# A gated recurrence with context: one accumulated state product, shorter chain, earlier place for the second direction

## The reference

```python
def hgrn2_scan(q, k, v, logf, s0, with_output):
    gcum = jnp.cumsum(chunks(logf), axis=2)
    g_end = gcum[:, :, -1]
    k_end = kc * jnp.exp(g_end[:, :, None] - gcum)
    chunk_states = jnp.einsum("bcshk,bcshv->bchkv", k_end, vc)
    s_final, s_in = lax.scan(_carry_step, s0, ...)        # s = dec * s + st
    if not with_output:
        return None, s_final
...
    q_rel = qc * jnp.exp(gcum - g_mid)
    k_rel = kc * jnp.exp(g_mid - gcum)
    att = jnp.where(causal, einsum(q_rel, k_rel), 0.0)
    o_intra = einsum(att, vc)
    o_inter = einsum(qc * jnp.exp(gcum), s_in)
    return o_intra + o_inter

# for each direction d (direction 1 on flipped tokens)
o_c, s_ctx = hgrn2_scan(qc_d, k_c, v_c, logf_c, s0, need_ctx)
o_l, _ = hgrn2_scan(q_l, k_l, v_l, logf_l, s_ctx, True)
```

## Time and profile before

| | us |
|---|---|
| median of 3 runs | 2481.95 (2480.68 to 2485.22) |
| profiled execution | 2486.94 |
| its span, first to last instruction | 2485.1 |
| rounds 3 to 7 of the loop, together | 136.10 |
| round 4 alone | 24.86 |

### The profile page before, as it was taken

One profiled execution on the slowest core, in us unless ns is written; L12 is line 12 of the kernel. 1 busy time (PEld: TensorE's weight loads), 2 busy tenths in 40 slices (PEclk: granted clock), 3 DMA queues, 4 the chain that ended last, 5 costly groups with the idle time before them and its releaser, 6 DMA issues. The chain is left out here.

```text
span 2485.1 us, 36625 instructions
## 1 busy us (share of the span) xinstructions
PE 2175.1 (88%) x12398; PEld 1790.4 (72%) x12398; DVE 1712.1 (69%) x2903; ACT 1366.1 (55%) x2135; POOL 277.2 (11%) x357
## 2 busy tenths in 40 slices
PE   5999899889998999888886799994889987799993
PEld 4899876589984666667575677783677786577782
DVE  5884626288555698977653699994478674699993
ACT  2663425166453355565333578883476652588882
POOL 0000000000000365555000001101000000001100
PEclk8999999999999999989997799996999887799996
DMA  6455431545543666400121699994221121699991
GB/s 219 162 186 170 142 109 45 203 158 190 175 135 145 250 222 239 162 1 1 43 84 51 230 389 389 390 386 177 94 77 59 52 85 60 219 394 398 393 371 68
DMA packets 127256, 454.99 MB, mean 183 GB/s; under 512 B 13824, under 2 KB 17792, under 8 KB 126976
## 3 DMA queue, kind: packets, MB, share of 16 engines
q1 hardware_dynamic: 116160, 413.14, 45.7%
q0 software_dynamic: 10944, 39.85, 4.2%
HBM read 431.97 MB, written 20.97 MB: 182 GB/s over the span
## 5 line engine op out<-in xcount | busy, mean ns | idle before, releaser
L2722 DVE TENSOR_TENSOR moe_w_lo<-ring,moe_w_hi 128x1024 fp32r<-128x1024 f32 x384 | 462.8, 1222 | 61.9 <-ACT moe_w_hi L2660 57.0
L2660 ACT CAST moe_w_hi<-ring 128x1024 fp32r<-128x1024 f32 x384 | 399.0, 1049 | 147.3 <-PE ps L236 119.4
L373 DVE TENSOR_TENSOR ffn_w_lo<-ring,ffn_w_hi 128x1024 fp32r<-128x1024 f32 x132 | 161.0, 1222 | 101.2 <-ACT ffn_w_hi L325 101.0
L234 PE MATMUL ps<-moe_w_hi,moe_own 128*128 128x512 f32 x512 | 213.8, 418 | 12.1 <-DVE moe_own L2729 11.1
L235 PE MATMUL ps<-moe_w_lo,moe_own 128*128 128x512 f32 x512 | 204.6, 400 | 0.0
L236 PE MATMUL ps<-moe_w_hi,moe_own 128*128 128x512 f32 x512 | 204.6, 400 | 0.0
L325 ACT CAST ffn_w_hi<-ring 128x1024 fp32r<-128x1024 f32 x132 | 137.4, 1044 | 107.4 <-PE ps L236 107.4
L234 PE MATMUL ps<-ffn_h_hi,ffn_w_hi 128*128 128x256 f32 x608 | 173.3, 285 | 11.2 <-DVE ffn_w_lo L373 11.2
L235 PE MATMUL ps<-ffn_h_lo,ffn_w_hi 128*128 128x256 f32 x608 | 172.0, 283 | 0.0
L236 PE MATMUL ps<-ffn_h_hi,ffn_w_lo 128*128 128x256 f32 x608 | 172.0, 283 | 0.0
L234 PE MATMUL ps<-ffn_hid,ffn_w_hi 128*128 128x256 f32 x448 | 131.1, 293 | 12.7 <-DVE ffn_w_lo L373 8.8
(11 more groups left out here) (541 smaller groups left out, 5692.0 us busy)
## 6 DMA issues: line engine op xcount, KB each, us to landing
ring<-in_weights SPq DMA_DIRECT2D x766, 512.0 KB, 5.4
expert_rows<-moe_y POOLq DMA_DIRECT2D x32, 512.0 KB, 7.1
token_rows<-moe_token_rows SPq DMA_DIRECT2D x6, 512.0 KB, 2.6
sq<-in_cmp_w SPq DMA_DIRECT2D x1, 2048.0 KB, 9.8
both<-in_x SPq DMA_DIRECT2D x1, 1024.0 KB, 5.8
both<-in_context SPq DMA_DIRECT2D x1, 1024.0 KB, 8.1
out<-both SPq DMA_DIRECT2D x1, 1024.0 KB, 4.8
cols<-in_cols SPq DMA_DIRECT2D x1, 720.5 KB, 9.1
```

What stands on the lines that cost most here:

```text
L234: pe.matmul(out, w_hi, x_hi, start=start, stop=False)
L373: dve.tensor_tensor(w_lo[:, u % WB], k.ring[:, (first + u) % RING], w_hi[:, u % WB], ALU.subtract).then_inc(w_split, 1)
L2660: act.copy(w_hi[:, j % WB].rearrange("p h f -> p (h f)"), k.slot(act, first + GU + j, e).rearrange("p a f -> p (a f)")).then_inc(w_rounded, 1)
L2722: dve.tensor_tensor(w_lo[:, j % WB].rearrange("p h f -> p (h f)"), k.ring[:, (first + GU + j) % RING].rearrange("p a f -> p (a f)"), w_hi[ ...
```

## The change

The context's state of a direction comes from one product over 256 tokens, in two accumulated matmuls of 128 tokens. For this the context's keys need the decay to the end of the context, not to the end of their chunk. `decays` therefore makes two scans: one over the latent half, restarted at each chunk, in place in `logs`, and one over 255 or 256 columns without restart that gives the decay to the end directly into `gs`; for direction 0 this second scan runs backwards through the columns, for direction 1 the first one does. The column at the end of the context is zero (cleared once). The latent half of `gs` then gets chunk end minus sum. The subtractions over 512 columns and the copy to `dec` go; `exps` reads the ends of the four latent chunks with a stride.

`carry` makes two matmuls of 128 tokens and three of 64 in place of seven of 64. `chain` makes one copy and three steps in place of one copy and six. On VectorE, `mask(h-2, 1)` and `chain(h-2, 1)` move in front of the split of `places[1]`.

```diff
@@ carry (TensorE)
+                        for a in range(2):
+                            pe.matmul(k.ps[:, STATE[0], 0:P], ket[:, d, a, :], v[:, a, h * P:(h + 1) * P], start=(a == 0), stop=(a == 1))
                         for c in order(d)[:-1]:
-                            a, r = c // 2, c % 2 * GC
-                            mm = pe.matmul(k.ps[:, STATE[c % 2], a * P:(a + 1) * P], ket[r:r + GC, d, a, :],
+                            a, r = 2 + c // 2, c % 2 * GC
+                            mm = pe.matmul(k.ps[:, STATE[c % 2], a * P - P:a * P], ket[r:r + GC, d, a, :],
                                            v[r:r + GC, a, h * P:(h + 1) * P], start=True, stop=True)
@@ exps (ScalarE)
-                        act.activation(ke[:, d, :], logs[:, d, :], ACT.Exp)
-                        act.activation(dec[:, h % 2, d, :], dec[:, h % 2, d, :], ACT.Exp)
-                        act.activation(qs[:, h % 2, d, :], gs[d][:, T:], ACT.Exp)
+                        act.activation(ke[:, d, :], gs[d][:, :], ACT.Exp)
+                        act.activation(dec[:, h % 2, d, :], chunk_ends(d), ACT.Exp)
+                        act.activation(qs[:, h % 2, d, :], logs[:, d, T:], ACT.Exp)
@@ before the loop (VectorE)
-                    dve.memset(sin[:, :, :, :], 0.0)
+                    dve.memset(gs[0][:, T - 1:T], 0.0)
+                    dve.memset(gs[1][:, 0:1], 0.0)
@@ decays (VectorE)
-                        dve.tensor_tensor_scan(gg[:, :], reset, L, 0.0, ALU.mult, ALU.add)
-                        dve.drain()
-                        chunks = gg[:, :].rearrange("p (c t) -> p c t", t=GC)
-                        dve.tensor_copy(own_dec, chunks[:, :, GC - 1])
-                        dve.drain()
-                        end = own_dec.unsqueeze(2).broadcast_to([P, 2 * NCH, GC])
+                        one = reset[:, 1:2].broadcast_to([P, T - 1])
                         if d == 0:
-                            dve.tensor_tensor(L.rearrange("p (c t) -> p c t", t=GC), end, chunks, ALU.subtract)
+                            dve.tensor_tensor_scan(sums, reset[:, T:], sums, 0.0, ALU.mult, ALU.add)
+                            dve.tensor_tensor_scan(to_end[:, 0:T - 1][:, ::-1], one, raw[:, 1:T][:, ::-1], 0.0, ALU.mult, ALU.add)
                             mid, edge = HC // 2 - 1, HC - 1
                         else:
-                            dve.tensor_tensor(L, gg[:, :], L, ALU.subtract)
-                            dve.drain()
-                            dve.tensor_tensor(chunks, end, L.rearrange("p (c t) -> p c t", t=GC), ALU.subtract)
-                            dve.drain()
+                            dve.tensor_tensor_scan(sums[:, ::-1], reset[:, T:], sums[:, ::-1], 0.0, ALU.mult, ALU.add)
+                            dve.tensor_tensor_scan(to_end[:, 1:T], one, raw[:, 0:T - 1], 0.0, ALU.mult, ALU.add)
                             mid, edge = HC // 2, HC
+                        dve.drain()
+                        dve.tensor_tensor(to_end[:, T:].rearrange("p (c t) -> p c t", t=GC), chunk_ends(d).unsqueeze(2).broadcast_to([P, NCH, GC]),
+                                          sums.rearrange("p (c t) -> p c t", t=GC), ALU.subtract)
@@ the rounds (VectorE)
-                        for n in places[1]:
-                            split(n + WB)
                         if live(h - 2):
                             mask(h - 2, 1)
                             chain(h - 2, 1)
+                        for n in places[1]:
+                            split(n + WB)
```

More of the change, by code:

```diff
@@ L2992, in odd_mixer @@
             rel = tb("hg_rel", [P, 2, 4, T])
-            dec = tb("hg_dec", [P, 2, 2, 2 * NCH])
+            dec = tb("hg_dec", [P, 2, 2, NCH])
             att = tb("hg_att", [P, 2, 2, P])
-            sin = tb("hg_s_in", [P, 2, NCH + 1, P])
+            sin = tb("hg_s_in", [P, 2, NCH, P])
             unit = tb("hg_unit", [P, 2 * GH - 1])
@@ L3024, in order, with chunk_ends @@
                 def order(d):
-                    ctx_ch = list(range(NCH))
-                    lat_ch = list(range(NCH, 2 * NCH))
-                    return (ctx_ch + lat_ch) if d == 0 else (ctx_ch[::-1] + lat_ch[::-1])
+                    return range(NCH) if d == 0 else range(NCH - 1, -1, -1)
+                def chunk_ends(d):
+                    at = GC - 1 if d == 0 else 0
+                    return logs[:, d, T:].rearrange("p (c t) -> p c t", t=GC)[:, :, at]
                 @block.sync
@@ L3110, in mix @@
                                           start=(d == 0 and a == 0), stop=False, skip_group_check=True)
-                            for i, c in enumerate(order(d)[NCH:]):
-                                cc = c - NCH
-                                mm = pe.matmul(k.ps[:, OUT, cc * GC:(cc + 1) * GC], sin[:, d, 1 + i, :],
+                            for i, cc in enumerate(order(d)):
+                                mm = pe.matmul(k.ps[:, OUT, cc * GC:(cc + 1) * GC], sin[:, d, i, :],
                                                qs[:, h % 2, d, cc * GC:(cc + 1) * GC], start=False, stop=(d == 1 and i == NCH - 1),
@@ L3334, in decays @@
                         u = 2 * h + d
-                        gg, L, own_dec = gs[d], logs[:, d, :], dec[:, h % 2, d, :]
+                        raw, to_end = logs[:, d, :], gs[d]
+                        sums = raw[:, T:]
                         dve.wait_ge(logged, u + 1)
@@ L3338, in decays @@
                             dve.wait_ge(expd, u - 1)
-                        dve.tensor_tensor_scan(gg[:, :], reset, L, 0.0, ALU.mult, ALU.add)
-                        dve.drain()
-                        chunks = gg[:, :].rearrange("p (c t) -> p c t", t=GC)
-                        dve.tensor_copy(own_dec, chunks[:, :, GC - 1])
-                        dve.drain()
-                        end = own_dec.unsqueeze(2).broadcast_to([P, 2 * NCH, GC])
+                        one = reset[:, 1:2].broadcast_to([P, T - 1])
                         if d == 0:
-                            dve.tensor_tensor(L.rearrange("p (c t) -> p c t", t=GC), end, chunks, ALU.subtract)
+                            dve.tensor_tensor_scan(sums, reset[:, T:], sums, 0.0, ALU.mult, ALU.add)
+                            dve.tensor_tensor_scan(to_end[:, 0:T - 1][:, ::-1], one, raw[:, 1:T][:, ::-1], 0.0, ALU.mult, ALU.add)
                             mid, edge = HC // 2 - 1, HC - 1
                         else:
-                            dve.tensor_tensor(L, gg[:, :], L, ALU.subtract)
-                            dve.drain()
-                            dve.tensor_tensor(chunks, end, L.rearrange("p (c t) -> p c t", t=GC), ALU.subtract)
-                            dve.drain()
+                            dve.tensor_tensor_scan(sums[:, ::-1], reset[:, T:], sums[:, ::-1], 0.0, ALU.mult, ALU.add)
+                            dve.tensor_tensor_scan(to_end[:, 1:T], one, raw[:, 0:T - 1], 0.0, ALU.mult, ALU.add)
                             mid, edge = HC // 2, HC
+                        dve.drain()
+                        dve.tensor_tensor(to_end[:, T:].rearrange("p (c t) -> p c t", t=GC), chunk_ends(d).unsqueeze(2).broadcast_to([P, NCH, GC]),
+                                          sums.rearrange("p (c t) -> p c t", t=GC), ALU.subtract)
                         for i, size, ref in ((0, GC, edge), (1, HC, mid)):
-                            own = gg[:, T:].rearrange("p (c t) -> p c t", t=size)
+                            own = sums.rearrange("p (c t) -> p c t", t=size)
                             refs = own[:, :, ref:ref + 1].broadcast_to([P, T // size, size])
@@ L3385, in chain @@
                         dve.wait_ge(states, 2 * h + d + 1)
+                        dve.tensor_copy(sin[:, d, 0, :], k.ps[:, STATE[0], 0:P])
                         for i, c in enumerate(order(d)[:-1]):
[L3387 to L3395, removed]
+                            dve.drain()
+                            ch = dve.scalar_tensor_tensor(sin[:, d, i + 1, :], sin[:, d, i, :], dec[:, h % 2, d, c:c + 1],
+                                                          k.ps[:, STATE[c % 2], (c // 2 + 1) * P:(c // 2 + 2) * P], ALU.mult, ALU.add)
                         ch.then_inc(chained, 1)
```

## The result

| | before | after |
|---|---|---|
| median, us | 2483.59 (4 runs, 2480.68 to 2486.85) | 2450.23 (4 runs, 2447.53 to 2455.03) |
| profiled execution, us | 2486.94 | 2447.53 |
| span, us | 2485.1 | 2445.8 |
| rounds 3 to 7, us | 136.10 | 109.57 |

The ratio is 0.9867, 95% interval 0.9844 to 0.9891: 33 us faster. The forecast was 2445, in a range of 2438 to 2463. (The same pair measured twice more: 0.9864, 0.9821 to 0.9908, and 0.9876, 0.9854 to 0.9897.)

What follows compares the result with a forecast made beforehand. Mix waited for VectorE's second-direction chain, late behind a split, with TensorE's low clock following the idle. Gains in rounds 2 to 9 summed to 36.8 us, giving 2450.1; minus 5.0 from profile to median, 2445, range 2438 to 2463.

Steps and rivals of the forecast that it cites:

- rounds 3 to 7: Five rounds at 21.75 us each instead of 136.10 us together, a gain of 27.35 us.
- Both halves are needed: VectorE's round: 22.65 us with the chain only moved, 23.7 with it only shortened, 18.6 us of work with both.
- round 9: The loop's round 9: a gain of 0.26 us; rounds 10 and after were to gain nothing.
- The carry: TensorE's carry with two 128-row and three 64-row products: 0.96 us, saving 0.13 per direction, 0.26 per round.
- Round 2: First carry 1.3 us earlier through ScalarE's queue, TensorE's work behind it 0.26 shorter; round 3's mix 4.7 us earlier.
- rival E: VectorE's backward scans are slow; the change loses from 4.3 us extra per scan, 2506 at 6 us; chance 0.03.
- The next bound: Once mix no longer waits: TensorE at 21.55 us a round or the loop through ScalarE at 21.74, nearly tied.
- rival B: TensorE's clock stays low in mix and attend even without the idle: gain 21.2 us, time 2461; chance 0.14.
- The step to the median: The median of the runs shown lay 5.0 us below the profiled execution; carried over, 2450.1 became 2445.
- Rival D: The wait is not relieved because VectorE reaches the mask late: gain under 5 us, 2477 to 2482; chance 0.03.
- C: A longer loop through ScalarE costs 1.5 us a round, 9 us over six rounds: 2454; chance 0.10.
- The slack of 3.6 us: VectorE finishes the second direction's mask and chain 17.9 us into the round; TensorE wants it at 21.5.

Runs made afterwards that it cites:

- the place alone: The kernel before with only mask and chain of direction 1 moved ahead of the second split, nothing shortened: 2456.37 us, 0.9874 of before.
- the shortening alone: The changed kernel with mask and chain of direction 1 put back behind the second split: 2471.48 us, 0.9929 of before.
- the Silu first: The changed kernel with ScalarE's Silu of the first tiles ahead of direction two's exponentials in rounds 8 and later: 2450.4 and 2447.8 us.
- the fourth product: The changed kernel with a fourth 64-row product per carry whose result nobody reads: 2452.02 us, 0.9858 of before.
- the idle put back: The changed kernel with fourteen clears of a scratch tile, each behind a drain, in the second direction's chain: 2523.75 us, 1.0156 of before.
- seven steps: The changed kernel with three more chained steps in each chain, results thrown away: 2453.13 us, 0.9866 of before.

## Why the prediction was right, step by step

**The bound.** Right. Mix waited for the second direction's chain and the chain for the split's cast: moving the chain alone removes the wait, and putting it back brings it back, at 1.72 to 2.01 us for a chain 1.2 us shorter. "Both halves are needed" was too strong: of the 34.8 us the place alone brings 31.6, the shortening alone 14.4.

**The sum**, by its own terms:

| step | forecast, us | measured, us |
|---|---|---|
| up to round 2's first carry | 1.3 | 1.29 |
| from there to round 3's mix | 3.4 | 2.40 |
| rounds 3 to 7 | 27.35 | 26.53 |
| round 8 | 4.5 | 4.95 |
| round 9 | 0.26 | -0.34 |
| sum | 36.8 | 34.83 |

Round 9 is longer than before although it was to gain. It begins at the low clock that round 8's wait of 2.93 us leaves behind, and the first group of mix takes 1.01 us where it takes 0.68 in the kernel with the Silu first; there the round takes 22.07 us, against 22.06 before the change.

**The carry** was mis-sized, in sign too: 0.96 us forecast against 1.09 before, 1.18 measured (1.28 for the first of a round, which starts right behind ScalarE's copy; in the kernel with the shortening alone, where it does not, the first takes 1.18 too). I priced a 64-row product at its mean, 0.156, though the prediction had weighed another rule and set it aside. The Trainium skill, page TensorE: Matmul & The Clock Gate, Part 3: Packing small matmuls, says that small products in different row groups run at the same time. The trace agrees: the fourth product is free, 0.65 us against 0.63. Counted in slots of a pair or a full product, the carry has four before and four after, and nothing is saved. Against the forecast this is 0.2 to 0.3 us per carry, some 0.5 a round. Little of it shows in rounds 3 to 7 (26.53 against 27.35), because I had taken 21.75 a round and not TensorE's 21.55.

**Round 2** gave 1.0 us less behind the carry. The work there ran at the low clock for longer than I had carried over: 0.72 over the 10 us from the carry on, where the kernel before has 0.78, with the carry itself at 2.31 us against 2.00.

**VectorE.** The sums take 1876.24 - 1873.32 = 2.92 us per direction (3.0 forecast). Forwards, a scan of 256 columns takes 0.69 us and one of 255 0.66 (the second direction's, L3351); backwards they take 0.68 (L3350) and 0.66 (L3347). Running backwards costs nothing here, so rival E falls. The first chain takes 1881.48 - 1880.03 = 1.45 (1.55). A gap of 0.43 in the second chain, put down to issue, lies within its slack.

**The next bound.** The forecast had TensorE at 21.55 and ScalarE's loop at 21.74, nearly tied. Measured is 21.92 for the round; with the carry's real price both come to about 22.0. ScalarE's loop leaves no gap: its exponentials wait 3.62 us for the second attend, from there it works without a pause up to its copy of the turned keys in the next round, and the first carry starts 0.05 us after that copy (1875.77 + 0.58 = 1876.35 against 1876.40). TensorE's last product in front of it starts at 1876.10, and such products start 0.12 apart, so TensorE has only some 0.2 us to spare there, as forecast.

```profile
1875.77 0.58 ACT L3214 ACTIVATE h<-ps 128x512 f32<-128x512 f32 x1
...
1884.80 0.63 ACT L3221 ACTIVATE h<-rstd 128x512 f32<-128x512 f32 x1 [3.62 <-PE ps L3088]
```

```profile
1876.10 0.28 PE L236 MATMUL ps<-hg_h_hi,hg_w_lo 128*128 128x256 f32 x1
```

The weight loads of the first carry show it as a wait in each of the five rounds:

```profile
PEld ps L3099 <- ACT h L3214: 1.1, 5, 0.2
```

**The clock, rival B**, did not come true: 1.00 in all five rounds. Its ground ("the falls need not be caused by the idle") falls with the idle put back. My counter-argument, that falls come right after idles of 2.9 us or more, held for the rows of before only: in the kernel with the shortening alone they follow idles of 1.72 to 2.01 us too, in three windows of six.

**The step to the median** was the weakest. The profiled execution of before was 5.0 us above the median of the runs shown, and I took that off the forecast. Without it the forecast would have been 2450.1, against 2450.2 measured; but that would be luck, errors that cancel: 2.0 us too much gain, a profiled run that stood 3.4 above the median of four runs, and medians that differ by 1.5 us less than the stage. With runs of one kernel 6 to 7.5 us apart, neither a median of three nor one trace is good to much less than 3 us here.

**Chances.** Rival D left no trace. Of C there is the loop through ScalarE, but at 21.92 a round and not 1.5 us above the forecast. The slack of 3.6 us for the moved chain was 3.5, in part by luck: the chain ended 18.4 us into the round (17.9 forecast), and mix wanted it at 21.9 (21.5).

## What to carry to other kernels

Look in a loop of several engines for the instruction that is needed first and stands behind one that waits for a later event; moving it cost nothing here and brought 31.6 of the 34.8 us. Count a bottleneck engine's idle with the slow stretch that follows it: here, with 3.1 us of idle a round, 5.3 went. And price small products by what runs at the same time, not by their mean.

## What the runs showed of the hardware

The lower clock of TensorE follows short idles, and not always. In the 8 us behind the eight idles of 4.8 to 5.8 us in the kernel with the idle put back, the granted clock was 0.50 to 0.57. In the kernel before, behind idles of 2.99 to 3.04 us, it was 0.57, 0.58, 0.58 and 0.79, but 1.00 behind one of 2.99, and 0.50 behind one of 3.62. Behind the six of 1.72 to 2.01 us in the kernel with the shortening alone it was 0.57 or 0.58 three times and 1.00 three times, at the same place of successive rounds. What decides between the two no run here shows. In rounds 3 to 7 of the changed kernel and of the ones with seven steps and with the fourth product, without idles in front of mix, it was 1.00 throughout.
